# The MLP's up projection by seven block products, with its result taken through memory to a down phase of its own

## What is computed

```
h = rmsnorm(x, p['norm_mlp'][layer])
x = x + (jnp.square(jax.nn.relu(h @ p['mlp_up'][layer])) @ p['mlp_down'][layer]).astype(dt)
```

## Time and profile before

| | |
|---|---|
| median of the runs | 3446.2 us |
| profiled execution: span (the page gives no other time) | 3447.1 us |
| PE busy | 3318.1 us, 96% |
| PE weight load busy | 3153.9 us, 91% |
| DVE busy | 1829.4 us, 53% |
| ACT busy | 828.4 us, 24% |
| POOL busy | 999.0 us, 29% |
| read from and written to memory | 166.57 and 32.57 MB |
| granted TensorE clock, mean | 0.984 |

### The profile page before, as it was taken

One profiled execution on the slowest core, in us unless ns is written; L12 is line 12 of the kernel. 1 busy time (PEld: TensorE's weight loads), 2 busy tenths in 40 slices (PEclk: granted clock), 3 DMA queues, 4 the chain that ended last, 5 costly groups with the idle time before them and its releaser, 6 DMA issues.

```text
span 3447.1 us, 74524 instructions
## 1 busy us (share of the span) xinstructions
PE 3318.1 (96%) x30180; PEld 3153.9 (91%) x30180; DVE 1829.4 (53%) x2984; ACT 828.4 (24%) x1751; POOL 999.0 (29%) x448
## 2 busy tenths in 40 slices
PE   7999889999999999999999989999999999999998
PEld 6998768888887899999999989999989999999998
DVE  5113864665666564444444474565556644444446
ACT  3344133333233222111111142222212211111112
POOL 3322210110013044333344423222212443333332
PEclk9999899999999999999999999999999999999999
DMA  5113630010012011111111111211231111111111
GB/s 167 57 62 99 192 114 12 23 35 15 24 35 85 27 53 50 49 43 43 49 49 49 43 37 50 70 57 60 73 125 35 56 49 43 43 49 43 43 49 69
DMA packets 81982, 200.20 MB, mean 58 GB/s; under 512 B 9225, under 2 KB 42677, under 8 KB 81625
## 3 DMA queue, kind: packets, MB, share of 16 engines
q1 hardware_dynamic: 37360, 121.39, 10.6%
q10 hardware_dynamic: 44392, 75.42, 6.4%
HBM read 166.57 MB, written 32.57 MB: 58 GB/s over the span
## 4 chain that ended last, share of the span: by engine, by line
PE 80%; DVE 5%; issue 1%; DMA 1%; ACT 1%; ACTq 0%; POOL 0%; DVEq 0%
PE psum L696 21%; PE psum L247 21%; PE psum L718 20%; PE psum L2117 2%; PE psum L3131 2%; PE psum L2134 1%; PE psum L1905 1%; PE psum L2091 1%; PE psum L2171 1%; PE psum L2104 1%; PE psum L2033 1%; PE psum L2137 1%; DVE s_sc L1571 1%; DMA act_lo<-c_lo 1%; DVE c_ks L3373 0%
## 5 line engine op out<-in xcount | busy, mean ns | idle before, releaser
L232 POOL TENSOR_TENSOR w_hi<-w_raw,derived 128x1024 fp32r<-128x1024 f32 x215 | 422.5, 1965 | 2284.0 <-PE psum L247 1327.3
L247 PE MATMUL psum<-act_hi,w_hi 128*128 128x352 f32 x2088 | 704.1, 337 | 28.8 <-DVE act_lo L342 12.1
L247 PE MATMUL psum<-act_hi,w_lo 128*128 128x352 f32 x2088 | 677.4, 324 | 0.0
L247 PE MATMUL psum<-act_lo,w_hi 128*128 128x352 f32 x2088 | 676.7, 324 | 0.0
L234 POOL TENSOR_TENSOR w_lo<-w_raw,w_hi 128x1024 fp32r<-128x1024 f32 x215 | 544.1, 2531 | 16.9
L803 DVE TENSOR_TENSOR x<-x,psum 128x352 f32<-128x352 f32 x768 | 387.3, 520 | 245.2 <-PE psum L718 240.6
L718 PE MATMUL psum<-ff_u_hi,w_hi 128*128 128x352 f32 x1536 | 496.6, 323 | 0.0
L696 PE MATMUL psum<-act_hi,w_hi 128*128 128x352 f32 x1536 | 495.9, 323 | 0.0
L718 PE MATMUL psum<-ff_u_lo,w_hi 128*128 128x352 f32 x1536 | 495.0, 322 | 0.0
L718 PE MATMUL psum<-ff_u_hi,w_lo 128*128 128x352 f32 x1536 | 494.8, 322 | 0.0
L696 PE MATMUL psum<-act_lo,w_hi 128*128 128x352 f32 x1536 | 492.3, 321 | 0.0
(11 more groups left out here) (470 smaller groups left out, 4440.3 us busy)
## 6 DMA issues: line engine op xcount, KB each, us to landing
w_raw<-weights SPq DMA_DIRECT2D x215, 512.0 KB, 3.3
s_cache<-cache_a ACTq DMA_DIRECT2D x32, 512.0 KB, 6.9
kv<-a_qkv ACTq DMA_DIRECT2D x12, 528.0 KB, 2.7
x<-x_in ACTq DMA_DIRECT2D x8, 528.0 KB, 5.1
y<-end_y SPq DMA_DIRECT2D x12, 352.0 KB, 2.4
c_S_s<-state_c ACTq DMA_DIRECT2D x8, 512.0 KB, 3.5
s_c<-c_S_s ACTq DMA_DIRECT2D x8, 512.0 KB, 2.7
out_raw<-mix ACTq DMA_DIRECT2D x7, 528.0 KB, 7.5
```

The costliest lines, as they stand in the source:

```text
L232: pool.tensor_tensor(hi, raw, self.zeros, ALU.add).then_inc(s.sem, s.step())
L247: last = pe.matmul(out, w[:, k, :], h[:, k, cols], start=(start and k == ks[0] and m == 0), stop=(stop and k == ks[-1] and m == 2))
```

## The change

- The up projection of a pair is a 2 x 2 block product: the weights of two hidden tiles, 8 input blocks, are cut in two halves of inputs and the two tiles; the tokens in two halves, each of 2 x HC columns (HC = 264). It is computed by seven products (Winograd's form) instead of eight: P1, P2, P6, P7, P5, P3, P4 in this order. Each has 4 input blocks x 3 fp32r products x 2 token pieces of 264 columns.
- Four of the seven weight blocks and four of the seven token operands are sums or differences. The weight sums S1 to S4 are made by DVE (512 columns each), for each pair; the high parts of all seven blocks by ACT, the low parts by POOL. The token operands (T1 to T4, and the quarters as they are) are made once per layer, during the output projection and the first pair.
- Products P1, P6, P5, P3 accumulate in PSUM banks 0 and 1; ACT copies the sum out after P1 (a), P6 (b) and P5 (c), and DVE adds a, b and c to the other banks' results: quadrants 11, 22, 12 and 21 of u.
- All 16 pairs of up come first. Each squared tile is stored to memory ("u", 32 x 128 x 1056). Then 16 groups of down load their two tiles of u again, ACT and DVE split them, POOL splits the down weights.
- There are no loops in the MLP any more. `Ahead` is gone; its work is in `MLP.act_rows` and `MLP.dve_step`.

```diff
-        self.head = [("up", 0)]
-        self.body = [("up", 1), ("down", 0), ("up", 0), ("down", 1)]
-        self.tail = [("up", 1), ("down", 0), ("down", 1)]
+    BLOCK = {1: 2, 2: 5, 6: 1, 7: 4, 5: 0, 3: 3, 4: 6}
+    BANK = {1: 0, 6: 0, 5: 0, 3: 0, 2: 2, 7: 4, 4: 4}
+    FRESH = (1, 2, 7)
...
+    def sp(self, sp):
...
+        for w in range(self.PAIRS):
+            tile = 2 * w + 2
+            if w == self.PAIRS - 1:
+                for q in range(2):
+                    u_load(0, q)
+            else:
...
+                sp.wait_ge(*at(f"split.{n}.{w}.lo4"))
+                raw(1, tile + 1)
+            if w < self.PAIRS - 2:
+                store(w, 0)
+                sp.wait_ge(*at(f"dve.{n}.{w + 1}.S4"))
+                sp.wait_ge(*at(f"split.{n}.{w + 1}.lo2"))
+                raw(0, tile + 2)
+                store(w, 1)
...
+        for g in range(1, self.GROUPS):
+            for q in range(2):
+                u_load(g, q)
+                sp.wait_ge(*at(f"split.{n}.d{g - 1}.lo{q}"))
+                raw(q, FF_TILES + 2 * g + q)
...
+        if m == 1:
...
+            dst, one, two, op = self.sums[0][:, :], a21, a22, ALU.add
+        elif m == 2:
...
+            dst, one, two, op = self.sums[1][:, :], self.sums[0][:, :], a11, ALU.subtract
+        elif m == 3:
+            self.block_free(dve, w, 7)
+            dst, one, two, op = self.weight(w, 7), a11, a21, ALU.subtract
...
+    def pool(self, pool):
...
+        for p in (1, 2, 6, 7):
+            self.weight_low(pool, 0, p)
+        pool.wait_ge(*at(f"pe.{self.out.n}.out{KC - 1}.{NT - 1}"))
+        for j in range(4):
+            pool.tensor_tensor(self.full(5, j), self.tokens(j, 1), self.tokens(j, 0), ALU.subtract)\
+                .then_inc(s.sem, s.step(f"split.{n}.T1_{j}"))
+        for p in (5, 3, 4):
+            self.weight_low(pool, 0, p)
...
+        def product(w, p):
+            hi, lo = self.block[p]
+            pe.wait_ge(*at(f"split.{n}.{w}.lo{p}"))
+            for tp in range(2):
+                if w == 0:
+                    self.operand_ready(pe, p, tp)
+                if p in self.FRESH:
+                    bank = self.BANK[p] + tp
+                    label = f"dve.{n}.{w - 1}.{ {1: 'r12', 2: 'q11', 7: 'q21'}[p] }" if w else self.emptied(bank)
+                elif p == 4:
+                    label = f"dve.{n}.{w}.q22"
+                else:
+                    label = f"act.{n}.{w}.{ {6: 'a', 5: 'b', 3: 'c'}[p] }{tp}"
+                pe.wait_ge(*at(label))
...
+        for w in range(self.PAIRS):
+            for p in (1, 2, 6):
+                product(w, p)
+            if w == 0:
+                self.pe_sum(pe)
+            for p in (7, 5, 3, 4):
+                product(w, p)
...
+        for w in range(1, self.PAIRS - 1):
+            keep_both(w, 0)
+            for p in (1, 2):
+                self.weight_high(act, w + 1, p)
+            self.square_out(act, w, "11")
+            keep_both(w, 1)
+            for p in (6, 7):
+                self.weight_high(act, w + 1, p)
+            keep_both(w, 2)
+            self.weight_high(act, w + 1, 5)
+            self.square_out(act, w, "22")
+            self.square_out(act, w, "12")
+            for p in (3, 4):
+                self.weight_high(act, w + 1, p)
+            self.square_out(act, w, "21")
...
+        self.quadrant(dve, 0, "11")
+        for tp in range(2):
+            dve.wait_ge(*at(f"act.{n}.hi_T4_{tp}"))
+            lo = self.far[:, :, 2, 1, tp]
+            dve.tensor_tensor(lo, self.far_full[:, :, 2, 1, tp], self.far[:, :, 2, 0, tp].bitcast(F32), ALU.subtract)\
+                .then_inc(s.sem, s.step(f"dve.{n}.lo_T4_{tp}"))
+        for w in range(self.PAIRS - 1):
+            if w:
+                self.quadrant(dve, w, "11")
+            for m in (1, 2, 3):
+                self.weight_sum(dve, w + 1, m)
+            self.quadrant(dve, w, "22")
+            self.quadrant(dve, w, "12")
+            self.weight_sum(dve, w + 1, 4)
+            self.quadrant(dve, w, "21")
+        w = self.PAIRS - 1
+        for where in ("11", "22", "12"):
+            self.quadrant(dve, w, where)
+        for q in range(2):
+            self.u_low(dve, 0, q)
+        self.quadrant(dve, w, "21")
```

More of the change, by code:

```diff
@@ L140 @@
 FF_TILES = 32
[L141 removed]
+TILES_C = 32
 class Kernel:
@@ L501, in act @@
         s = K.plan.steps["act"]
[L503 to L534, removed]
@@ L536, in low, with keep_both @@
-    def low(self, dve, k, c=None):
+        def keep_both(w, m):
+            for tp in range(2):
+                self.keep(act, w, m, tp)
+        self.act_rows(act)
+        keep_both(0, 0)
+        for j in range(4):
+            act.wait_ge(*at(f"split.{n}.T1_{j}"))
+            act.activation(self.high(5, j), self.full(5, j), ACT.Copy, scale=self.gain_of(j))\
+                .then_inc(s.sem, s.step(f"act.{n}.hi_T1_{j}"))
+        self.weight_high(act, 0, 5)
+        self.weight_high(act, 0, 3)
@@ L537, in low, with dve_step @@
+        for t in range(self.after.STEPS + self.after.LATE + 1):
+            self.after.act_step(act, t)
+    def dve_step(self, dve, k, c):
         K, n, at = self.K, self.n, self.K.plan.at
         s = K.plan.steps["dve"]
[L539 to L544 removed]
@@ new lines, in dve_step @@
+        if (k, c) == (6, 1):
+            self.weight_sum(dve, 0, 1)
+            self.weight_sum(dve, 0, 2)
+        if (k, c) == (7, 0):
+            self.weight_sum(dve, 0, 3)
+        if 4 <= k < 7 and c == 2:
+            mixed(k - 4)
+        if k < 7 or c == 0:
+            return
+        mixed(3, c - 1)
+        if c == 1:
+            return
+        dve.wait_ge(*at(f"act.{n}.hi7.1"))
+        low_row(7)
+        for p, name in ((6, "T2"), (7, "T3")):
+            dve.wait_ge(*at(f"act.{n}.hi_{name}_3.1"))
+            lower(p, 3, name)
@@ new lines, in quadrant @@
+        p, kept, label, before = {"11": (2, 0, "a1", "21"), "22": (7, 2, "c1", "11"), "12": (3, None, None, "22"),
+                                  "21": (4, 1, "b1", "12")}[where]
+        dve.wait_ge(*at(f"pe.{n}.{w}.P{p}.1"))
+        if w or before != "21":
+            dve.wait_ge(*at(f"act.{n}.{w - 1 if before == '21' else w}.sq{before}"))
+        src = self.bank(p)
+        if kept is not None:
+            dve.wait_ge(*at(f"act.{n}.{w}.{label}"))
+            dve.tensor_tensor(self.r[:, :, :], src, self.kept[kept][:, :, :], ALU.add).then_inc(s.sem, s.step(f"dve.{n}.{w}.q{where}"))
+            dve.wait_ge(*at(f"dve.{n}.{w}.q{where}"))
+            src = self.r[:, :, :]
```

758 lines of the change are left out of this document (465 added, 293 removed).

## The result

| | before | after |
|---|---|---|
| median of the runs, us | 3446.34 | 3406.03 |
| lowest and highest, us | 3441.04, 3451.81 | 3403.55, 3413.17 |
| ratio, 95% interval | | 0.9887 (0.9873 to 0.9900) |
| profiled execution: time, span, us | | 3413.17, 3411.4 |
| read, written, MB | 166.57, 32.57 | 201.17, 67.17 |

The change is faster by 34 to 44 us. The time lies in the range given (3364 to 3430). Of the cases, rival (a), a fixed overhead per matmul (3410 us), is what happened, not the forecast itself.

A forecast was written before the change was run, and what follows sets the result against it. TensorE's matmuls were taken to bound the kernel. Per layer -45.8 + 15.4 + 2.3 + 1.5 = -26.6 us, -53.2 for two; 3447.1 - 53.2 - 0.9 = 3393.0 us, range 3364 to 3430.

The forecast's parts named there:

- rival (a): Up matmuls: overhead per matmul stays fixed, 122.3 ns each, 16.6 us more in all, 3410 us; chance 0.12.
- Up matmuls: Up phase: 168 matmuls of 264 columns at 119.2 ns, a pair 20.03 us instead of 22.89; -45.8 us a layer.
- The other bound, 122.3: Up matmuls: ns each if the overhead stays a fixed 12.3 ns; 8.3 us a layer less gain.
- First pair: First up pair of a layer: late operands and a slower clock, less the old head's 2.1 us; net +15.4 us a layer.
- the walk: First pair, product by product: waits before P2, P3 and P4, quadrant 22 at about 31.5 us, end at 34.5 to 35.1.
- Rival (b): First pair is cheap, costing only +3 us a layer: 3368 us in all; chance 0.10.
- Up to down: Between the phases: first down matmul waits for the first two u tiles; +2.3 us a layer, bounds 1 and 6.
- Steady pair: Later up pairs: occasional wait of P3 on copy c0, 0.7 us spare, 0.1 us a pair; +1.5 us a layer.
- (d): Steady pairs bound by the chain P7, S3, hi7, c0, P3: 2 to 3 us a pair, 3455 to 3480 us; chance 0.09.
- (e): Steady pairs partly bound by that same chain: 0.5 to 1.2 us a pair, 3410 to 3430 us; chance 0.12.
- (f): Down phase stalls because u tiles return late from memory: about 3450 us; chance 0.02.
- Down groups, code, memory traffic: Down phase stays at 22.96 us a group, straight code and u tiles through memory add nothing: cost 0.

The follow-up runs named there:

- experiment 5: Changed kernel with the up matmuls streaming only 256 of the 264 columns of each token piece; 3384.2 us (one run).
- experiment 12: Changed kernel with the up matmuls reading one weight column broadcast over 128 (stationary operand with step 0); 3402.03 us (one run).
- experiment 7: Changed kernel with all up matmuls using 64 of the 128 rows, 264 columns as before; 3900.13 us (one run).
- experiment 3: Changed kernel with POOL's four T1 differences made to wait for DVE's low part of row 7; 3407.25 us, ratio 0.9890 to the kernel before.
- experiment 9: Changed kernel with POOL's four T1 differences left out, P5 using one half of the tokens as it is; 3397.72 us (one run).
- experiment 10: Changed kernel with DVE doing the weight sum S3 twice in pairs 1 to 15; 3411.34 us (one run).

## Why the prediction was right, and where it was not

- **Up matmuls.** Forecast 119.2 ns and -45.8 us a layer; measured 122.0 and -38.4. This is the term that was mis-sized, by 7.4 us a layer, 14.8 in all, more than the whole distance from 3393 to 3406. The step that failed is "all lie on 0.452 to 0.461 ns a column": it made a ratio of a distance that is columns / 2.4 plus about 12 ns (352, 264 and 256 columns, experiment 5), and leaned on a stretch of four matmuls, misread by 2 ns (experiment 12). Its own 115 at 256 columns is 0.449 and lies outside the range it names. The other bound, 122.3, was written down beside it, and held to 0.3 ns. The 512-column matmuls of the same rows, at 236 ns, have 23 ns over their 213, so they fitted neither rule. The Trainium skill (TensorE: Matmul & The Clock Gate, section Back-to-back issue gap) has 2.5 ns over the columns at full clock, for a matmul by itself; here, where each has its own weight load, it is 11 to 12 at 256, 264 and 352 columns. The Trainium skill's rule for half clock in the same section, columns / 1.2, agrees with the 220.1 ns of experiment 7.
- **First pair.** Forecast 35.1 + 2.4 of clock = 37.5; measured 36.9 and 36.7, net +14.3 and +14.1 for +15.4. In the first layer the waits of P2 (2.3 forecast, 2.1 measured), P3 (1.4 and 0.8) and P4 (6.6 and 6.5) are each where the walk had them; in the second P2's is twice as long (4.7), P3's is nil and P4's 5.8. What bore it is that DVE's and POOL's operations add: experiment 3 shows that moving POOL's gains nothing, experiment 9 that quadrant 22 comes 4.3 and 3.2 us sooner with 5.0 us of them left out. Rival (b) is out. Some of the agreement is luck. The walk priced the slower clock behind P4 alone, but P2 lost 1.6 us to it as well; and it had 4.0 us for the row sums and their logarithm (10.9 to 14.9), where 2.0 were needed (12.6 to 14.7), so that P7 began on time. Its "about 31.5" for quadrant 22 leaves out the 0.6 at its start: 0.6 + 20.3 + 11.2 = 32.1. And the stall that it calls 8 us is a wait of 6.3 us in the trace.
- **Up to down.** Forecast +2.3; measured 2.2, and in the first layer 1.6 more for a clock that fell behind it. The prediction had no price for a clock that falls there.
- **Steady pair.** Forecast +1.5 a layer; measured 0. The chain's times in the trace of the changed kernel:
```profile
1443.99 0.69 DVE L684 TENSOR_TENSOR ff_w_full<-ff_raw,ff_raw 128x512 f32<-128x512 f32 x1 [1.91 <-PE psum L770]
...
1444.72 0.63 ACT L697 ACTIVATE ff_w_hi<-ff_w_full 128x512 fp32r<-128x512 f32 x1 [1.98 <-DVE ff_w_full L684]
1445.45 0.39 ACT L902 ACTIVATE ff_c<-psum 128x264 f32<-128x264 f32 x1
1446.94 0.39 ACT L902 ACTIVATE ff_c<-psum 128x264 f32<-128x264 f32 x1 [1.09 <-PE psum L770]
```
  S3, hi7 and c0 follow one another as walked, c0 done at 1445.84, 0.89 us before P3 begins (1446.74); c1 waits for P5's second chunk and begins 1.1 us after c0's end. (The slower matmuls themselves add a little slack.) Experiment 10 puts an operation of 0.69 us on the chain, and nearly every pair hides it. (d), (e) and (f) are out.
- **Down groups, code, memory traffic.** Forecast 0; measured 22.96 us a group and no wait between the first group and the last ones, with 34.6 MB more read and written each over the kernel. The end of the first layer's down phase, forecast unchanged, takes 1.0 us more.

With 122.0 ns in place of 119.2 and nothing else changed, the forecast's sum is -19.2 a layer, and 3408 us. That this is within 2 us of the result owes something to terms that cancel: the first pair and the steady pairs cost some 1 us and 1.5 us a layer less than forecast, the clock behind the first layer's last up 1.6 us more and the end of its down phase 1.0 more.

## What to carry to other kernels

Split the distance of short matmuls into columns over clock plus a fixed part, fitted on long rows of them, before pricing a change of width; seven products instead of eight are worth 10.5% of the up time here (20.49 for 22.89 us) and not 12.5%, and only while the distance stays above its floor. Where DVE and POOL share a stretch without free time, their operations add, so only removing work or putting the result that is waited for first shortens it, and every later waiter must be walked again after such a reordering. A slack that is worked out per pair can be tested at once, by doubling one operation on its chain; its size is then read from the time between the end of the chain and the start of what waits for it, pair by pair, and not from the total. And a distance between instructions is taken from their starts, not from a span less a duration.

## What the runs showed of the hardware, beside what was expected

- Distance of fp32r matmuls at full clock: 159.0 ns (352 columns), 122.0 (264), 118.2 (256), 111.7 to 111.9 (192). With a stationary operand that repeats one column: 120.6 (264).
- At half granted clock the overhead is gone: 220.1 ns at 264 columns, 264 / 1.2 = 220.0.
- With 64 rows in every matmul, PE 100% busy, the granted clock stayed at 0.50 for 560 us of the up phase; with 64 rows in one product of seven it stayed at 1.00. The distance at full clock is the same for 64 and 128 rows, but each change from one to the other costs about 0.2 us.
- A wait of PE of 2.2 us was followed by some 4 us at 0.57 in one MLP and by none at 1.00 in the other, of the same execution. The old head's hole of 2.1 us had no fall of the clock behind it (34.36 us for 216 matmuls).
